# Down weights requested slice by slice, and two FFN tiles transposed by DMA

## The reference

```python
def swiglu_ffn(h, w_gate, w_up, w_down):
    g = jnp.einsum("bsd,df->bsf", h, w_gate.astype(h.dtype))
    u = jnp.einsum("bsd,df->bsf", h, w_up.astype(h.dtype))
    return jnp.einsum("bsf,fd->bsd", jax.nn.silu(g) * u, w_down.astype(h.dtype))
...
        x = x + rmsnorm(swiglu_ffn(rmsnorm(x, ffn_pre_g), w_gate, w_up, w_down), ffn_post_g)
```

## Time and profile before

| | |
|---|---|
| median of 3 executions | 901.28 us (900.07 to 927.17) |
| the profiled execution | 901.29 us |
| its span on the slowest core (core 0) | 899.8 us |
| spans of the other cores | 895.4 to 898.1 us |
| PE busy | 858.9 us, 95% of the span, in 4936 matmuls |
| ACT, DVE, POOL busy | 306.8, 390.4, 127.3 us |
| share of PE in the chain of work that ended last | 91% |

### The profile page before, as it was taken

The page is one execution under the profiler, slowest core; times in us unless marked ns, Lnnn a source line. Parts: engine busy times, 40 slices in busy tenths (PEclk is TensorE's granted clock), DMA queues, the critical chain, the costliest instruction groups (busy, mean ns, idle before and its releaser), DMA issues.

```text
span 899.8 us, 13332 instructions; the slowest of 8 cores (895.4 to 899.8 us)
## 1 busy us (share of the span) xinstructions
PE 858.9 (95%) x4936; PEld 437.0 (49%) x4936; DVE 390.4 (43%) x500; ACT 306.8 (34%) x552; POOL 127.3 (14%) x293
## 2 busy tenths in 40 slices
PE   1899999999999999999799999999999999999997
PEld 1657444465764455554344444444444444444443
DVE  1477758347457678876331123231232222212122
ACT  2332446432546667764231111331012320111101
POOL 3121113121113224221310000000000000000000
PEclk9999999999999999999899999999999999999999
DMA  9599058359893456977793014010121101210011
GB/s 192 151 172 193 1 187 273 122 98 159 162 232 58 71 164 170 199 148 187 176 203 67 1 70 141 24 47 1 71 92 73 47 1 47 78 64 0 1 47 70
DMA packets 25312, 95.85 MB, mean 107 GB/s; under 512 B 2944, under 2 KB 3072, under 8 KB 24480
## 3 DMA queue, kind: packets, MB, share of 16 engines
q0 software_dynamic: 7776, 33.03, 23.3%
q1 hardware_dynamic: 17472, 61.97, 20.1%
HBM read 107.05 MB, written 20.97 MB: 142 GB/s over the span
## 4 chain that ended last, share of the span: by engine, by line
PE 91%; ACT 3%; DMA 2%; DVE 1%; issue 1%; POOL 1%; DVEq 0%; SPq 0%; POOLq 0%; ACTq 0%
PE pp L374 87%; PE pp L433 4%; ACT t L354 3%; DMA t<-x 2%; DVE t L367 1%; DVE t L1003 1%; POOL t L377 0%; POOL t L1124 0%; SPq L377 0%; DVE t L357 0%; ACT L354 0%; DVEq L1189 0%; POOL t L357 0%; DVE t L371 0%; POOLq L1189 0%
## 5 line engine op out<-in xcount | busy, mean ns | idle before, releaser
L374 PE MATMUL pp<-t,t 128*128 128x512 bf16 (+2 forms) x4272 | 827.7, 355 | 3.8 <-ACT t L354 2.7
L374 PEld LDWEIGHTS pp<-t,t 128*128 128x128 bf16 x4272 | 397.1, 98 | 410.6 <-issue 9.1
L357 DVE TENSOR_TENSOR t<-pp,t 128x512 bf16<-128x512 f32 (+4 forms) x173 | 150.4, 873 | 370.2 <-PE pp L374 199.3
L354 ACT ACTIVATE t<-pp 128x512 f32<-128x512 f32 (+5 forms) x216 | 161.6, 760 | 359.2 <-PE pp L374 323.4
L367 DVE SCALAR_TENSOR_TENSOR t<-t,t,t 128x1024 bf16<-128x1024 f32 (+4 forms) x100 | 126.6, 1271 | 58.2 <-POOL t L357 36.9
L361 POOL TENSOR_SCALAR t<-t 128x1 f32<-128x1 f32 (+2 forms) x102 | 24.6, 241 | 634.2 <-ACT t L354 329.4
L433 PE MATMUL pp<-t,t 128*128 128x128 bf16 (+1 forms) x664 | 48.5, 223 | 30.3 <-DVE t L367 27.1
L354 ACT ACTIVATE pp<-pp 128x1024 f32<-128x1024 f32 (+1 forms) x17 | 16.3, 958 | 142.3 <-PE pp L374 142.3
L433 PEld LDWEIGHTS pp<-t,t 128*128 128x128 bf16 (+1 forms) x664 | 42.3, 100 | 44.9 <-issue 34.6
L357 POOL TENSOR_TENSOR t<-t,t 128x1 f32<-128x1 f32 (+2 forms) x103 | 60.6, 589 | 15.3 <-POOL t L361 0.2
L354 ACT ACTIVATE t<-pp,t 128x256 bf16<-128x256 f32 (+2 forms) x76 | 44.0, 584 | 42.8 <-DVE t L1003 34.2
(11 more groups left out here) (27 smaller groups left out, 60.9 us busy)
## 6 DMA issues: line engine op xcount, KB each, us to landing
t<-x SPq DMA_DIRECT2D x68, 512.0 KB, 6.9
x<-t SPq DMA_DIRECT2D x24, 512.0 KB, 3.8
t<-w_gu POOLq DMA_DIRECT2D x22, 512.0 KB, 7.3
out<-t SPq DMA_DIRECT2D x15, 512.0 KB, 2.8
t<-w_dn POOLq DMA_DIRECT2D x6, 768.0 KB, 17.2
t<-gains SPq DMA_DIRECT2D x6, 512.0 KB, 10.5
t<-w_ing POOLq DMA_DIRECT2D x8, 256.0 KB, 17.9
t<-w_inc POOLq DMA_DIRECT2D x4, 512.0 KB, 10.1
```

The lines of the kernel that those rows point to most:

```text
L354: S.op("act", lambda e: e.activation(out=out, in_=in_, func=func, **kw), reads, writes)
L357: S.op(eng, lambda e: e.tensor_tensor(out=out, in0=in0, in1=in1, op=op), reads, writes)
L374: S.op("pe", lambda e: e.matmul(out, lhsT=lhsT, rhs=rhs, start=start, stop=stop), reads, writes, signal)
```

## The change

Three things change, all in the FFN stage.

1. The seven requests for down weights ahead of the FFN loop are gone, with the wait on `x20`. All 22 pieces are requested inside tile 0: four pieces in one transfer behind slice 3, and three pieces in one transfer behind each of the slices 4 to 9. `wdn` replaces `wd3`.
2. The request for the gain `G4` moves from ahead of the loop to behind slice 12 of tile 0.
3. For tiles 2 and 3 (prepared during tiles 1 and 2) `t_3` is not called. Directly behind `prep3`, a DMA transpose of `hs` to the tile buffer `h3` is issued on SP (`dmaT`, which existed as a helper). Tile 1 is transposed by TensorE as before.

```diff
-        dma("sp", "G4", G4[:], gain_d[GN_FFPOST], [], ["G4"])
         while gul:
             gload()
-        for j in range(4):
-            wload("wd%d" % j, wd[:, j], wd_d[:, j], ["wd%d" % j], ["x20"])
-        def wd3(j):
-            S.dma("pool", "wd%d" % j, lambda e: e.dma_start(out=wd[:, j:j + 3, :], in_=wd_d[:, j:j + 3, :]),
-                  [], ["wd%d" % k for k in range(j, j + 3)])
-
-        for j in (4, 7, 10):
-            wd3(j)
+
+        def wdn(j, n):
+            S.dma("pool", "wd%d" % j, lambda e: e.dma_start(out=wd[:, j:j + n, :], in_=wd_d[:, j:j + n, :]),
+                  [], ["wd%d" % k for k in range(j, j + n)])
+
+        WDL = {3: [(0, 4)], 4: [(4, 3)], 5: [(7, 3)], 6: [(10, 3)], 7: [(13, 3)], 8: [(16, 3)], 9: [(19, 3)]}
...
                 if t + 1 < NF:
                     if jj in (3, 6, 9, 12) and t > 0:
                         load3((t + 1) * 4 + jj // 3 - 1, jj // 3 - 1)
-                    if jj - 2 in p3:
-                        t_3((t + 1) * 4 + p3.index(jj - 2), hs3, "act")
+                    if jj - 2 in p3 and t == 0:
+                        t_3(4 + p3.index(jj - 2), hs3, "act")
                     if jj in p3:
-                        hs3 = prep3((t + 1) * 4 + p3.index(jj))
-                if t == 0 and jj in (7, 8, 9):
-                    wd3(13 + 3 * (jj - 7))
+                        k = p3.index(jj)
+                        hs3 = prep3((t + 1) * 4 + k)
+                        if t > 0:
+                            dmaT("h3T%d" % k, h3[(t + 1) % 2][:, :, k * 128:(k + 1) * 128], hst[hs3], ["hs%d" % hs3],
+                                 ["g%d_%d" % ((t + 1) % 2, k)])
+                if t == 0 and jj in WDL:
+                    for j0, n in WDL[jj]:
+                        wdn(j0, n)
+                if t == 0 and jj == 12:
+                    dma("sp", "G4", G4[:], gain_d[GN_FFPOST], [], ["G4"])
```

## The result

The changed kernel takes **888.55 us** (median of 4, 888.23 to 889.61); forecast were 889.0 with a range of 886 to 895. Beside the kernel before on the same chip its ratio is 0.9866, with a 95% interval of 0.9851 to 0.9882: 1.3% faster. (The median of before in that comparison, 913.99 us, lies between two executions at 900.07 and 901.28 and two at 926.7 and 927.17, in a slower state that the ratio leaves out.) So the 25.4 us between the two medians are not what the change is worth; by the ratio it is 12.1 us. Later runs of the kernel before gave medians of 901.3 to 901.5. Measured twice more beside other kernels, the ratio was 0.9865 and 0.9872.

What follows compares the result with a forecast made beforehand. The kernel was taken as bound by PE nearly everywhere (TensorE 91% of the chain). 8.8 us from the down weights and 3.6 from the transposes make 12.4; 901.3 - 12.4 = 889 us, range 886 to 895.

Steps and rivals of the forecast that it cites:

- both terms of the sum: On PE in the FFN: 8.8 us from the down weights' requests moved, 3.6 us from TensorE transposes removed.
- faster by over 2% (about what a measurement of this kernel can tell from no change): Whole kernel: a time below 883.3 us, given 3%; 93% went to between 883.3 and 919.3.
- core 0 sets the time still: Core 7, 4.4 us ahead by span, gains 6.6 and stays ahead by over 2, so core 0's gain counts.
- the wait's cause: First FFN block: PE idles 6.48 us because POOL's root stands behind seven down-weight requests, the first awaiting a load.
- The clock behind the wait: Behind PE's first FFN wait: TensorE at 1.2 GHz after standing idle loses 2.28 us, regained without the wait.
- The 64 transposes: Tiles 2 and 3: eight groups of eight leave PE, 0.45 us each, 3.6 us in all.
- Landing of the weights: Down weights, requested from about 440.5 on, land by 488; the down projection begins at 500.9, 13 us left.
- T of a transpose: Time of one 256 KB DMA transpose on SP in the FFN, taken as 8.2 us or less.
- The threshold: Tiles 1 and 2: late transposes make ACT wait from T = 13.7 us, PE from T = 18.3, by 2T - 36.6 per tile.
- SP's loads behind a transpose: nothing: SP's list in the FFN: loads behind a transpose are wanted at least 18 us later, against 6.9 to land; no cost.
- the slow rival: DMA transposes over 18.3 us each stall ACT, then PE; at 27.9 each the kernel takes 927 us; 6%.
- 4T - 73.2: PE's stall in us over two tiles if one DMA transpose takes T, above 18.3; gain eaten at T = 21.4.

Runs made afterwards that it cites:

- the one run where the `hs` buffer was the limit: Changed kernel with each DMA transpose done eight times, and the next tile's four block loads requested ahead of all transposes on SP: 914.17 us, ratio 1.0144.
- eight repeats: Changed kernel with each DMA transpose done eight times over into the same place, each waiting for the one before: 925 us, ratio 1.0261.

## Why the prediction was right, and where it was not

The mechanism and both terms of the sum held. The step that failed is the one from the sum to the chances: "faster by over 2% (about what a measurement of this kernel can tell from no change)", by which 93% went to a time between 883.3 and 919.3, as if 1.4% could not be told from nothing. The runs showed an interval of 0.15% to either side of a ratio of 0.9866. In the account by core, "core 0 sets the time still" failed too.

- **What bounds, and the wait's cause.** Shown: both the load (the wait of 5.06 to 6.98 fell to 1.76 without it) and the issuing (the 1.76 left) held the root, and with both away the wait is zero on every core.
- **The clock behind the wait.** Shown: on core 0 9.63 us between the first two groups became 7.36 with the wait gone, and 7.35 on the slowest core with the wait shortened to 1.76.
- **The 64 transposes.** Shown in place: 0.45 a group left the chain. Measured alone the part is 2.8 us with an interval of 1.6 to 4.1 that holds the forecast 3.6.
- **Landing of the weights.** They end before 485, forecast by 488; no wait at the down projection.
- **T of a transpose was mis-sized.** 8.2 us was taken, from the one load of 256 KB on SP; the loads of 256 KB on POOL, with medians of 9.6 to 17.9 us, were passed over. T is 2.8, close to the other end, the store of 256 KB at 2.0. It decides nothing, as all but the 17.9 are under the 13.7 from which ACT would wait, and that one is under the 18.3 from which PE would. The estimate of 10.5 from the Trainium skill ("VectorE: DVE Perf Modes", The three transpose paths: eight at 1309 ns) is nearly four times what this trace has on quiet queues.
- **The threshold.** 2T - 36.6 per tile held to 0.5 us in the one run where the `hs` buffer was the limit. But "SP's loads behind a transpose: nothing" was said for the T taken and carried over to the slow rival unchanged: a transpose slow enough to matter also holds back the loads behind it, and with T at 23 that, not the buffer, set the time: eight repeats cost 36 us, where 4T - 73.2 at 23 gives 19. So its price of 38 us at 27.9 was most likely too low; no run had that T.
- **"Core 0 sets the time still" failed.** The longest cores are 7 and 4, and core 0 is among the shortest: 887.4 was forecast for its span, it took 884.4, and 887.0 is core 7's. That the sum made from core 0 met the time is in part luck. From the first transposes to the last norm core 0 and core 7 take the same 443.91 us (434.13 to 878.04, 436.76 to 880.67); they differ by when they enter the FFN, and that order is not a core's own: core 7 was ahead of core 0 by 2.4 us before, and 2.6 us behind it now. The price on core 0 was right, the ranking built on one execution was not. The forecast time came out close because the latest core entered the FFN at nearly the same moment in both executions (436.91 and 436.76).
- **"About what a measurement of this kernel can tell" failed.** No row was given for the 2%, and two of the three executions of before, 900.07 and 901.28, lie 0.13% apart. Half the interval of the ratio is 0.15%, so a change of 1.3%, which was forecast in microseconds, is clear of noise nine times over. The forecast's weight stood on "within 2%", which is where the number lies, but it reads as if no difference were to be seen; the line to draw was "faster, by 1.4%".

## What to carry to other kernels

In an in-order queue, what a tiny instruction waits behind counts, not what it costs: here 0.8 us of POOL's work stood behind seven DMA requests, and PE paid the wait and then the slow clock. Where a DMA replaces compute, look first at what shares its queue and its engines in that stretch: the same transpose landed in 2.8 us on quiet queues, in 8 beside weight loads, in 25 to 41 behind a burst of them. And a request without a wait of its own goes out when its engine is free, not where the code puts it.

## What the runs showed of the hardware

- A DMA transpose of 128x1024 bfloat16 within SBUF landed in 2.8 us on quiet queues, and a row of them, each waiting for the last, had nearly the same pace (32 issued in 91.6 us, 2.9 each). SP needed 1.22 us to issue one, and up to 15 us on full queues.
- Small packets come with it: those under 512 B went from 2944 to 11344 by the two pages, 1050 for each of the eight transposes.
- After a wait of 1.76 us TensorE ran on at its 2.4 GHz level; after the waits of 5.06 to 6.98 us the next transposes took 1.01 us instead of 0.61, and on core 0 they and the first matmuls behind them ran at 1.2 GHz (granted clock 0.50 from 441 to 446).
